# A shifted bias table kept as 32 copies in DRAM instead of 128, and read by four transfers a block

## The reference, cut to what matters

```
def t5_bias(table, dist):
    n = jnp.maximum(dist, 0)
    ...
    return table.astype(jnp.float32)[bucket]

bias = t5_bias(table, q_pos[None, :, None] - idx)
logits = jnp.where(valid[:, :, None, None, :], logits + bias, NEG)
```

## Time and profile before

| What | Value |
|---|---|
| Median of three runs | 1207.48 us (1204.01 to 1210.04) |
| The profiled execution's own time | 1207.71 us |
| Its span in the trace | 1206.0 us |
| TensorE busy | 1162.5 us, 96% |
| VectorE busy | 891.5 us, 74% |
| ScalarE busy | 558.5 us, 46% |
| GpSimd busy | 91.9 us, 8% |
| Mean granted TensorE clock | 0.993 |
| DMA traffic | 132.38 MB, of which 9.79 MB are written to DRAM |
| Writing of bias_skewed | 4 DMAs of 1,280 KB |
| Reading of bias_skewed | 4 DMAs of 1,024 KB and one of 2,048 KB |

### The profile page before, as it was taken

The page is one execution under the profiler, slowest core; times in us unless marked ns, Lnnn a source line. Parts: engine busy times, 40 slices in busy tenths (PEclk is TensorE's granted clock), DMA queues, the critical chain, the costliest instruction groups (busy, mean ns, idle before and its releaser), DMA issues.

```text
span 1206.0 us, 24762 instructions
## 1 busy us (share of the span) xinstructions
PE 1162.5 (96%) x9294; PEld 1068.5 (89%) x9294; DVE 891.5 (74%) x1759; ACT 558.5 (46%) x1012; POOL 91.9 (8%) x141
## 2 busy tenths in 40 slices
PE   7999989999999999999999999899999999999995
PEld 3959845589999999999999988699999999999995
DVE  2279989847899588587677766778896795795676
ACT  2342148753664353343334566745652443543334
POOL 4424400200000000000410000000000000000000
PEclk9999999999999999999999999999999999999998
DMA  7699590044223223223433221042223332233222
GB/s 213 177 279 293 156 271 3 10 151 123 70 71 106 87 88 123 87 86 125 144 100 106 78 69 38 26 149 71 71 71 123 87 106 91 85 105 105 88 88 71
DMA packets 64048, 132.38 MB, mean 110 GB/s; under 512 B 7835, under 2 KB 36667, under 8 KB 63819
## 3 DMA queue, kind: packets, MB, share of 16 engines
q1 hardware_dynamic: 47899, 115.16, 30.4%
q10 hardware_dynamic: 12688, 9.31, 2.6%
q0 software_dynamic: 3360, 6.56, 1.7%
HBM read 126.46 MB, written 9.79 MB: 113 GB/s over the span
## 4 chain that ended last, share of the span: by engine, by line
PE 80%; DVE 15%; ACT 2%; issue 2%; DMA 0%; SPq 0%; ACTq 0%; DVEq 0%
PE PS L703 34%; PE PS L900 20%; PE PS L735 12%; PE PS L1206 3%; PE PS L1018 2%; PE PS L978 2%; DVE SC L2464 2%; PE PS L963 2%; PE PS L992 2%; DVE MX L2462 2%; DVE PB L2290 1%; DVE MSK L2473 1%; PE PS L1118 1%; DVE YA L2149 1%; PE PS L1038 1%
## 5 line engine op out<-in xcount | busy, mean ns | idle before, releaser
L703 PE MATMUL PS<-XH,WHI 128*128 128x260 f32 x1088 | 221.6, 285 | 0.7 <-DVE XL L2333 0.7
L703 PE MATMUL PS<-XH,WLO 128*128 128x260 f32 x1088 | 219.1, 283 | 0.0
L703 PE MATMUL PS<-XL,WHI 128*128 128x260 f32 x1088 | 218.8, 283 | 0.0
L703 PEld LDWEIGHTS PS<-XH,WHI 128*128 128x128 f32 x1088 | 167.5, 188 | 5.9 <-issue 4.8
L703 PEld LDWEIGHTS PS<-XH,WLO 128*128 128x128 f32 x1088 | 167.7, 188 | 0.0
L703 PEld LDWEIGHTS PS<-XL,WHI 128*128 128x128 f32 x1088 | 167.3, 188 | 0.0
L1268 ACT ACTIVATE WHI<-WRAW 128x1024 fp32r<-128x1024 f32 x72 | 76.2, 1059 | 177.8 <-PE PS L703 146.0
L1810 DVE TENSOR_TENSOR WLO<-WRAW,WHI 128x1024 fp32r<-128x1024 f32 x64 | 80.0, 1249 | 98.5 <-ACT WHI L1268 98.5
L900 PE MATMUL PS<-HH,RNH 128*128 128x260 f32 x384 | 109.1, 284 | 2.5 <-DVE RNL L1950 2.4
L900 PE MATMUL PS<-HH,RNL 128*128 128x260 f32 x384 | 108.4, 282 | 0.0
L900 PE MATMUL PS<-HL,RNH 128*128 128x260 f32 x384 | 108.3, 282 | 0.0
(11 more groups left out here) (349 smaller groups left out, 2798.8 us busy)
## 6 DMA issues: line engine op xcount, KB each, us to landing
WRAW<-wall SPq DMA_DIRECT2D x168, 512.0 KB, 3.6
bias_skewed<-bias_seq SPq DMA_DIRECT2D x4, 1280.0 KB, 17.1
BT<-bias_skewed ACTq DMA_DIRECT2D x3, 1024.0 KB, 9.1
X<-xT SPq DMA_DIRECT2D x4, 520.0 KB, 7.0
X<-xT SPq DMA_DIRECT2D x1, 2080.0 KB, 11.3
yT<-X SPq DMA_DIRECT2D x8, 260.0 KB
KVB<-cacheK SPq DMA_DIRECT2D x16, 128.0 KB, 3.2
KVX<-cacheK SPq DMA_DIRECT2D x16, 128.0 KB, 3.1
```

Of the source, the lines that this page charges most:

```text
L703: mm = pe.matmul(PS[:, 2 * slot + g, 0:TG], tile, x[:, k, TG * g:TG * g + TG], start=(k == 0 and w is w_hi and x is hi), stop=(k == KT - 1 ...
```

## The change

`bias_skewed` becomes 32 x 16 x 768 values, written by one DMA of 32 copies. Rows i0 to i0+31 of a block, for i0 = 0, 32, 64 and 96, are read from the same 32 copies at a column offset that is i0 smaller. So every read becomes four DMAs of 32 partitions each. The semaphores' counts go with it: `toe_skew` to 16, `toe_in[t]` and `bt_back` to 64. The compute instructions are the same.

```diff
-SKEW = 768
+SKEW, QUART = 768, 32
...
-        bskew = nc.dram_tensor("bias_skewed", [P, NH, SKEW], F32, kind="Internal").ap()
+        bskew = nc.dram_tensor("bias_skewed", [QUART, NH, SKEW], F32, kind="Internal").ap()
...
+        def bias_columns(eng, to, c0, c1, done):
+
+            for i0 in range(0, P, QUART):
+                eng.dma_start(to[i0:i0 + QUART], bskew[:, :, 127 - i0 + c0:127 - i0 + c1]
+                              ).then_inc(done, 16)
...
-            for i0 in range(0, P, 32):
-                sp.dma_start(bass.AP(tensor=bskew.tensor, offset=i0 * (NH * SKEW + 1),
-                                     ap=[[NH * SKEW + 1, 32], [SKEW, NH], [1, 640]]),
-                             bass.AP(tensor=bseq.tensor, offset=0,
-                                     ap=[[0, 32], [640, NH], [1, 640]])).then_inc(toe_skew, 16)
+            sp.dma_start(bass.AP(tensor=bskew.tensor, offset=0,
+                                 ap=[[NH * SKEW + 1, QUART], [SKEW, NH], [1, 640]]),
+                         bass.AP(tensor=bseq.tensor, offset=0,
+                                 ap=[[0, QUART], [640, NH], [1, 640]])).then_inc(toe_skew, 16)
             early(POOL_LO[0] // 2, 1)
-            sp.wait_ge(toe_skew, 16 * 4)
+            sp.wait_ge(toe_skew, 16)
             sp.wait_ge(is_relu, 3 * IDXH)
             sp.wait_ge(ds_mm, 3)
-            sp.dma_start(BT0[:], bskew[:, :, 127 + 384:127 + 512]).then_inc(toe_in[0], 16)
+            bias_columns(sp, BT0[:], 384, 512, toe_in[0])
...
                     if m == 0 and layer == 0:
-                        act.dma_start(BT[:, :, 256:512], bskew[:, :, 127 + 256:127 + 512]
-                                      ).then_inc(bt_back, 16)
+                        bias_columns(act, BT[:, :, 256:512], 256, 512, bt_back)
...
             def load_bias(t):
                 c0, c1 = 384 - P * t, 512 - P * t
-                act.dma_start(BT[:, :, c0:c1], bskew[:, :, 127 + c0:127 + c1]
-                              ).then_inc(toe_in[t], 16)
+                bias_columns(act, BT[:, :, c0:c1], c0, c1, toe_in[t])
```

More of the change, by code:

```diff
@@ L601, in _ @@
             sp.wait_ge(kv_used, 2 * DB)
-            sp.wait_ge(toe_in[3], 16)
+            sp.wait_ge(toe_in[3], 16 * 4)
             sp.wait_ge(lo_pool, LO_PIECES * LO_SKIP)
@@ L681, in _ @@
                 low_part(u, u % 2)
-            pool.wait_ge(bt_back, 16)
+            pool.wait_ge(bt_back, 16 * 4)
             for h in range(NH):
@@ L1700, in load_bias @@
                 c0, c1 = 384 - P * t, 512 - P * t
-                act.dma_start(BT[:, :, c0:c1], bskew[:, :, 127 + c0:127 + c1]
-                              ).then_inc(toe_in[t], 16)
+                bias_columns(act, BT[:, :, c0:c1], c0, c1, toe_in[t])
             act.wait_ge(kv_used, DB)
-            act.wait_ge(toe_in[0], 16)
+            act.wait_ge(toe_in[0], 16 * 4)
             nc.scalar.activation(BT[:, :, 384:512], BT0[:], ACT.Copy).then_inc(bt_copy, 1)
@@ L1713, in _ @@
                                  ACT.Copy).then_inc(dt_ev, 1)
-            act.wait_ge(toe_skew, 16 * 4)
+            act.wait_ge(toe_skew, 16)
             load_bias(1)
@@ L2281, in softmax_in @@
                     if not sink:
-                        dve.wait_ge(toe_in[t], 16)
+                        dve.wait_ge(toe_in[t], 16 * 4)
                         if t == 1:
```

## The result

The changed kernel took 1212.72 us as the median of 16 runs (1207.29 to 1218.55), the kernel before 1207.62 us (16 runs, 1202.13 to 1214.11). The ratio is 1.0046 with a 95% interval of [1.003, 1.0062]: slower by 5.1 us, within the 0.5% of the forecast and inside its range, but clearly not the 0 us that the sum gave. A second set of four runs gave 1.0069 [1.0044, 1.0093]. The profiled execution took 1218.55 us, the slowest of the sixteen, so its trace shows the losses larger than usual; a second profile, of an execution that took 1216.04 us, is used beside it.

The account below looks back on a forecast made before the run. It took TensorE, busy 96% of the span, as the bound, with 0% DMA on the chain. All terms cost 0, leaving 1207.7 us, forecast as 1207.5 us from the runs' median; range 1200 to 1216 us.

Parts of the forecast that it names:

- no change within 0.5%: Whole kernel: a time within 0.5%, 6.0 us, of the kernel before; chance 0.83.
- four zeros: The sum on the path, 0 + 0 + 0 + 0, giving 1207.7 us against the profiled execution.
- The writes: Bias writes on SyncE: four DMAs become one, 3.9 MB less traffic, the 0.6 us wait ahead of BT0 goes.
- Rival D: Freed DMA time is worth something: three waits go, 7.8 us, hence 1199.9 us; chance 0.06.
- BT0 and unit 10, "Cost 0": SyncE: BT0's four issues delay unit 10's load by 1.2 us, covered by 1.7 us of slack; cost 0.
- "the same time": Bias loads: a transfer to 32 partitions taken to last as long, given the same 512-byte runs and total.
- load_bias(1), "Cost 0": ScalarE from 161.76 us: three more issues hidden by 3.02 us idle, data 3.7 us early for VectorE; cost 0.
- load_bias(2) and (3), "Cost 0": ScalarE: eight issues take 4.8 us from 172.37 to 177.2, just fitting 5.00 us idle before PTB; cost 0.
- The lower bound: ScalarE's eight issues: the old 1.94 us stall is waiting for room, so more issues add nothing to it.
- The reload in the MLP: ScalarE at 577.98 us: three more issues of 0.53 us end at 580.1, before next work at 580.79; cost 0.
- Rival B: ScalarE: each fourth issue takes 3.45 us, PTB late, 1213.0 us; decides once the eight issues exceed 7 us; chance 0.09.
- Rival C: Narrow loads take twice as long, delaying unit 10 and bias block 1: 9.7 us, 1217.4 us; chance 0.06.

Follow-up runs that it names:

- kernel 4: Kernel before with one write of 32 copies, each read one 128-partition transfer from overlapping rows (other bias values): 1206.47 us, ratio 0.9999.
- kernel 1: Kernel before, its 128 copies and four writes kept, each read split into four transfers of 32 neighbouring partitions: 1215.8 us, ratio 1.008.
- kernel 9: Kernel before, 128 copies and four writes kept, only BT0's load split into four transfers of 32 partitions: 1211.44 us, ratio 1.0055.
- kernel 6: Changed kernel with load_bias(2) and (3) issued by SyncE instead of ScalarE: 1209.21 us, ratio 1.0022 to the kernel before.
- kernel 2: Kernel before, 128 copies and four writes kept, each read split by heads into four transfers of all 128 partitions: 1208.94 us, ratio 1.0024.
- kernel 3: Changed kernel with copies shifted by 4b, each transfer landing on 32 partitions in steps of four: 1209.6 us, ratio 1.0033 to the kernel before.
- kernel 10: Kernel before, 128 copies and four writes kept, only ScalarE's bias loads split into four transfers of 32 partitions: 1212.25 us, ratio 1.0051.

## Why the prediction was right, and where it was not

The range held the time, and "no change within 0.5%" held by the ratio of the first set, 1.0046; the second set, 1.0069, lies outside it. The sum behind it did not hold: four zeros stood for 5.1 us. So the forecast of no change held by the width of its bound and not by its mechanism, and that is luck.

- **The writes.** Right. SyncE's wait went, and the freed DMA time by itself is worth 0 (kernel 4). Rival D is refuted for this kernel with wide reads. In company of narrow reads the smaller write may help: kernel 1, with the old writes, has 1.008, the change 1.0046 and 1.0069.
- **BT0 and unit 10, "Cost 0".** The cover did not hold, but the loss is small. The issue term was right (unit 10's load issued 1.0 and 1.3 us later, 1.2 predicted). The failed step is the landing: "the same time" for a narrow transfer. Behind a narrow BT0, unit 10's load took 8.4 to 11.3 us to land (10.5 and 9.5 in the two profiles, 10.8 and 11.3 in kernels 1 and 9, 8.4 in kernel 6); behind BT0 loads of the other forms it took 7.0 to 9.1 (before, kernels 2, 3, 4 and 10). Unit 10's high part came 2.4 and 1.7 us later than before and used up the slack of 1.7 us. TensorE waited 1.98 and 1.07 us in the two profiles, yet it started unit 10 only 0.67 and 0.04 us later than before, and in kernel 6's profile it did not wait for it at all.
- **load_bias(1), "Cost 0".** Its own data came in time, and the exponentials were covered. But the step counted only who waits for this transfer and not who shares the engines with it: the V pages beside it. They were in no term of the sum; this is a path that the prediction left out.
- **load_bias(2) and (3), "Cost 0".** Wrong in two numbers, and the term that is shown to cost time. The eight issues took 6.3 and 6.5 us, not 4.8: six at about 0.65 and the last two longer, 0.94 and 1.34 in the chain above. And the cover of 5.4 us was read as a time that begins with the issues. It ends at what VectorE and TensorE do, whose clock runs on while V pages are late; in kernel 6 only 2.66 us of it were left. The lower bound, that the stall of 1.94 us would not grow with more issues, was an assumption that no row showed; 1.5 to 1.7 us came on top of the 4.8. The step from the change to kernel 6, 1.0046 (or 1.0069) to 1.0022, is about 3 us or more, the largest step that one move of the changed kernel gave, and it fits the 3.7 and 3.9 us by which the issues held up PTB.
- **The reload in the MLP.** Right. Four issues took 2.74 us, and ScalarE's next work began 2.85 us after their start, where it had been 2.81.
- **Rival B** named the right place and the right victim, but its mark, "over 7 us", was too high; the stall was spread over the issues and not 3.45 us in every fourth.
- **Rival C** had the mechanism that the change and kernels 1 to 3 show, with 0.06 as its chance. "The rows tie the time to the run length and not to the partitions" was an argument from silence: no row had a bias load on 32 partitions at all. Its size was too large: 1.55 times, not twice, and VectorE did not wait for block 1 of the bias in either profile. The Trainium skill's port rule, set aside there, was the better guide.

What remains open is how the 5 us of the change divide between late V pages and the issues behind them, and what unit 10 adds; the intervals of 0.15% do not resolve steps of one us, and the single profiles differ by about as much.

## What to carry to other kernels

Before splitting a transfer by partitions, ask which partitions each piece reaches: pieces in steps of four over all 128, or pieces of the free dimension, kept the full rate here, and neighbouring 32 did not. Each additional issue took some 0.65 to 0.8 us here on the stream that made it. Read its cover by when the next work becomes ready, not as the idle time of the old trace, and ask what else may come late ahead of it. A wait that appears in the new trace is not yet a loss: compare when the work behind it starts. The 3.9 MB saved where no engine waited for a transfer were worth nothing measurable by themselves (kernel 4).

## What the runs showed of the hardware that was not expected

- Eight transfers on 32 neighbouring partitions each moved 187 GB/s at full DMA engines, where two transfers on 128 moved about 290, with the same runs of 512 bytes. Transfers on 32 partitions in steps of four moved near 290.
- The rate was as low with 128 copies as the source (kernel 1: 189 GB/s from 176.5 to 187 us) as with 32, so it does not come from the number of copies that are read.
- DMA engines at a share of 1.08 moved only 248 GB/s (104 to 114 us in the change): the share alone does not say that much is being moved.
